# A keyed attention in a two-part network: an opening with fewer fill products and the longest tile, and token shifts moved from GpSimd into the gaps of a search on VectorE

## The chip, the cores and the metric

The kernel is one launch on one core of a Trainium2 chip. Five engines run side by side, each with its own instruction order, and meet through semaphores: TensorE (PE, matrix products into PSUM), VectorE (DVE), ScalarE (ACT), GpSimd (POOL) and SyncE (SP, which only issues transfers here). The metric is the device time of the launch in microseconds. The time before is 4012.95 us, the median of three runs (4010.0 to 4013.63).

## The reference

All arrays are float32, 1024 tokens by 1024 features. A first block (a gated mixer and an MLP) is followed by two layers of a second block, each of which runs three branches from one input product. The change touches the branch that attends to chosen keys, and the token shift of the recurrent branch, in both layers:

```python
def token_shift_mix(z, mu):
    prev = jnp.pad(z, ((0, 0), (1, 0), (0, 0)))[:, :-1]
    return z + (prev - z) * mu

# recurrent branch: r, k, v, g and two low-rank inputs are columns of z after the shift
kk = k * k_k
kk = kk / max(norm(kk, per head of 64), 1e-12)

# chosen keys, for each block of 128 queries
sc = einsum(relu(iq . ik * 32 ** -0.5), iw)         # 8 index heads of 32
sc = where(key <= query, sc, -inf)
_, idx = top_k(sc, 256)                             # the first of equal scores win
att = q . k[idx] * 64 ** -0.5                       # 4 heads of 64, one k and v for all
out = softmax(where(idx <= query, att, -inf)) . v[idx] * silu(g)
```

The kernel gathers nothing. It finds, for each query, the 256th largest score by halving an interval 32 times, makes from it a mask over all keys (0 for chosen, a huge negative number for the rest), and attends densely under the mask.

## The kernel before

Rows (tokens) lie on the 128 partitions, so there are NT = 8 tiles of 128 tokens. The phases follow each other with a barrier of all engines between them. For each of the two layers: `win2`, `dsa_attend`, `rwkv`, `dilated`, `tail`.

**`win2`, the input stage.** TensorE multiplies the normed input by twelve chunks of weight columns in the order of `WIN_CHUNKS` (L3298), 8 tiles a chunk, 8 products a tile. Most chunks are 384 columns wide, `low` is 128. Chunks 0 to 3 also feed the index scores `sc`. ScalarE evicts each tile from PSUM into one of two slots of `ot` (`evict`, L3458); a chunk may be evicted into a slot only when the chunk two before it is stored. SyncE loads the weights two chunks ahead, and for each finished chunk from 4 on stores it to DRAM (L3391). The chunks v, g, low, r and k (4, 6, 8, 9, 10) are first shifted: SyncE copies the chunk one token down into `zp` by four transfers (L3384 to L3387), and `shift` (L3340) computes z + (zp - z) * mu in three passes over the whole chunk. The first four of these run on GpSimd (L3520 to L3524), the last, k, on VectorE. ScalarE then applies SiLU to g and tanh to half of low (`shape`, L3492), at fixed places of its order.

VectorE sums the index scores (`add_heads`), and from about 1720 us of the span runs the search (`dsa_search`, L2456): a loop of BISECT = 32 trips, each with six counts over the score tiles 2 to 7 (384 to 1024 wide; tiles 0 and 1 need no choice, as all their keys are taken) and six small instructions on 128x6. Behind the search come the shift of k, the product with k_k, its square and the sum per head, then (after ScalarE's square root) the normalised `kk`, whose store closes the phase.

**`dsa_attend`, the attention.** `TILE_ORDER` is 0, 1, 7, 6, 5, 4, 3, 2; each tile has four heads, 32 units `m` in all. TensorE makes the scores of unit m + 2 (L2554), then turns unit m by transposes (L2563) and multiplies by v (L2574). VectorE adds the mask and takes the row minimum (`attend`, L2657), ScalarE takes the exponential and copies the turned blocks. The mask of a tile is made in parts: `choose` on VectorE (L2632: keys above the upper limit, candidates between the limits, a running count by a scan, the first of them up to the number needed), one part behind each unit, and the last two passes on GpSimd (L2620, L2621). `keep_busy` (L2542) issues fill products whose results are never read: 16 at the start, and 2 or 8 behind the heads of the first two tiles, 34 calls. Each call is two records in the trace, as float32 products are.

Of the kernel before, what the change touches and what calls it, by code (L numbers as in the profile page):

```python
# [2455 lines left out]
def dsa_search(ph, B, sc, junk):  # L2456
# [6 lines left out]
    def search(dve):  # L2463
        s = Steps(dve, step, 0, PRE)

# [9 lines left out]
        with dve.Fori(0, BISECT) as i:  # L2475
            s = Steps(dve, step, 0, PER)
            s.base = PRE + i * PER
# [12 lines left out]
    return search  # L2490


TILE_ORDER = list(range(T0)) + list(range(NT - 1, T0 - 1, -1))


def dsa_attend(nc, A, S, l_, hT, Z, L_, B, sc):
# [3 lines left out]
    with Phase(nc, "datt") as ph:  # L2500
        room = Z["room"]
        ident, causal = L_["ident"], B["causal"]
        gt, pre, mask = (carve(room, q * 2 * SEQ, [2, SEQ]) for q in range(3))
        cand, ones = room[:, 6 * SEQ:7 * SEQ], room[:, 7 * SEQ:8 * SEQ]
# [8 lines left out]
        ones_set, step, gstep, made, masked, expd, turned, pT_ready, o_made, inv_ready, o_read, row_done, chosen, mask_ready = (  # L2513
            ph.sem(n) for n in ("ones_set step gstep made masked expd turned pT_ready o_made inv_ready o_read row_done chosen "
                                "mask_ready").split())
# [7 lines left out]
        with ph.block() as block:  # L2523
# [17 lines left out]
            def _(pe):  # L2541
# [36 lines left out]
                def busy_after(m):  # L2578
                    i, h = m // DSA_H, m % DSA_H
                    if i < 2 and h < DSA_H - 1:  # L2580
                        keep_busy(i % 2, 8 if m == 2 * DSA_H - 2 else 2)

                scores(0)
                scores(1)
                keep_busy(0, 16)
                k = 0
                for m in range(NM):
                    if m + 2 < NM:
                        scores(m + 2)
                    while k < len(groups) and groups[k][0] == m:  # L2590
                        turn(k)
                        if k >= 1:
                            values(k - 1)
                            if groups[k - 1][0] != m:
                                busy_after(m - 1)
                        k += 1
                values(k - 1)

            @block.gpsimd
            def _(gp):  # L2600
                count = [0]

                def s(ins):
                    count[0] += 1
                    ins.then_inc(gstep, 1)
                    gp.wait_ge(gstep, START + count[0])

                gp.memset(ones[:, :], 1.0).then_inc(ones_set, 1)
                for i, t in enumerate(TILE_ORDER):
                    L, j = (t + 1) * P, i % 2  # L2610
                    mk = mask[:, j, :]
                    if i >= 2:
                        gp.wait_ge(masked, START + DSA_H * (i - 1))
                    if t < T0:
                        if t > 0:
# [1085 lines left out]
```

## Time and profile before

| | us |
|---|---|
| median of three runs | 4012.95 |
| profiled execution | 4015.7 |
| its span, first to last instruction | 4014.4 |
| TensorE busy | 3644.9 (91%) |
| VectorE busy | 2205.6 (55%) |
| ScalarE busy | 1133.7 (28%) |
| GpSimd busy | 506.2 (13%) |
| mean granted TensorE clock | 0.953 of full |

The two input stages and the two attentions take about 1565 to 2043 and 2045 to 2155 us in the first layer, 2793 to 3277 and 3279 to 3388 us in the second. In a timeline a line is the start in us, the duration in us, the engine and the line of the code, the operation, the tiles written and read, their shapes and the number of instructions merged, and in brackets the idle time of the engine before it with what ended it.

### The profile page before, as it was taken

Reading aid. Unit: us, or ns where it says so; the run is one execution under the profiler, and the core shown is the slowest. Engines: PE = TensorE matmul, PEld = TensorE weight load, DVE = VectorE, ACT = ScalarE, POOL = GpSimd, SP = SyncE. Lnnn points to the kernel's source line nnn. Section 1 sums busy time; section 2 is a strip of 40 time slices with the busy share of each in tenths; the row PEclk is TensorE's granted clock in tenths of the full one; section 3 lists DMA queues with packets and bytes.
Section 4 is the critical chain, followed back from the end, with each engine's and each line's share of the span. In section 5 each row is a group of like instructions: output and inputs, shape, how many; then the busy total and the mean of one; then the engine's idle time right before and its main releaser. Section 6 shows DMA issues by size and latency. Waiting matters only on the chain. (4 is left out here: it accounts for less than half of the span.)

```text
span 4014.4 us, 58104 instructions
## 1 busy us (share of the span) xinstructions
PE 3644.9 (91%) x22944; PEld 2327.5 (58%) x22944; DVE 2205.6 (55%) x4609; ACT 1133.7 (28%) x2429; POOL 506.2 (13%) x314
## 2 busy tenths in 40 slices
PE   5999848799999997999997997998999988898898
PEld 4555424685478544656665885444655655787444
DVE  3143476446764573589865553342389875653343
ACT  2121135221122011411134555222320114555222
POOL 0010033000110010012211111110002211121110
PEclk7999969899999998999998998999999999998899
DMA  6332322323433452123331204111013341202220
GB/s 216 137 115 88 109 101 79 116 95 147 177 117 105 147 185 86 32 63 93 111 108 50 72 20 164 49 65 57 27 56 92 105 137 52 59 30 102 94 77 23
DMA packets 234283, 377.16 MB, mean 94 GB/s; under 512 B 30742, under 2 KB 163870, under 8 KB 233014
## 3 DMA queue, kind: packets, MB, share of 16 engines
q1 hardware_dynamic: 234030, 373.58, 28.2%
q8 instruction: 184, 3.01, 0.3%
q14 instruction: 69, 0.57, 0.0%
HBM read 290.84 MB, written 69.08 MB: 90 GB/s over the span
## 5 line engine op out<-in xcount | busy, mean ns | idle before, releaser
L3413 PE MATMUL win_acc<-across_room,across_hT 128*128 128x384 f32 (+3 forms) x3072 | 907.8, 456 | 3.7 <-PEq L83 3.7
L3413 PEld LDWEIGHTS win_acc<-across_room,across_hT 128*128 128x128 f32 x3072 | 561.0, 191 | 345.1 <-issue 15.0
L2480 DVE TENSOR_SCALAR_CACHE_REDUCE win_rl<-d_sc,win_mid 128x384 f32<-128x384 f32 (+5 forms) x384 | 363.2, 946 | 35.9 <-DVE win_mid L2488 24.0
L3252 PE MATMUL tail_wo<-tail_w_out,across_room 128*128 128x512 f32 x512 | 230.1, 604 | 9.3 <-issue 9.3
L453 PE MATMUL zin_acc<-zin_wt,across_hT 128*128 128x512 f32 (+2 forms) x640 | 229.2, 513 | 0.0
L3263 PE MATMUL tail_wg<-tail_w_gate,across_room 128*128 128x512 f32 x512 | 225.3, 594 | 1.0 <-DVE across_room L3093 1.0
L3474 ACT ACTIVATE d_ot<-win_acc 128x384 f32<-128x384 f32 (+1 forms) x144 | 66.9, 466 | 562.8 <-PE win_acc L3413 562.7
L453 PEld LDWEIGHTS zin_acc<-zin_wt,across_hT 128*128 128x128 f32 x640 | 119.9, 190 | 98.3 <-issue 88.6
L3252 PEld LDWEIGHTS tail_wo<-tail_w_out,across_room 128*128 128x128 f32 x512 | 98.0, 194 | 129.0 <-issue 129.0
L1700 PE MATMUL mlp_bk<-across_hT,across_room 128*128 128x256 f32 x768 | 171.0, 379 | 0.0
L3263 PEld LDWEIGHTS tail_wg<-tail_w_gate,across_room 128*128 128x128 f32 x512 | 96.5, 191 | 116.5 <-issue 116.5
L1700 PEld LDWEIGHTS mlp_bk<-across_hT,across_room 128*128 128x128 f32 x768 | 145.9, 190 | 19.8
L3345 POOL TENSOR_TENSOR win_zp<-win_zp,d_ot 128x3072 f32<-128x3072 f32 (+1 forms) x8 | 44.8, 5605 | 824.0 <-DMA win_zp<-s_z 824.0
L2318 PE MATMUL rwkv_bk<-rwkv_Tb,rwkv_PS 64*64 64x64 f32 x1920 | 128.0, 220 | 7.6 <-DVE rwkv_PS L2075 7.6
L2316 PE MATMUL rwkv_bk<-rwkv_PS,rwkv_Tb 64*64 64x64 f32 x1536 | 113.4, 224 | 17.2 <-DVE rwkv_PS L2075 17.2
L1700 PE MATMUL mlp_bk<-mlp_tsums,mlp_sums 128*128 128x256 f32 x512 | 117.6, 383 | 10.8 <-DVE across_room L1428 9.3
L2075 DVE TENSOR_TENSOR rwkv_PS<-rwkv_bk,layer_early 128x128 f32<-128x128 f32 x240 | 67.9, 288 | 104.5 <-PE rwkv_bk L2305 103.2
L1387 POOL TENSOR_TENSOR mlp_t<-mlp_t,mlp_rows 128x1024 f32<-128x1024 f32 x8 | 20.2, 2526 | 791.8 <-ACT mlp_t L1634 791.8
L1249 PE MATMUL mid_wo<-across_room,mid_yT 128*128 128x512 f32 x256 | 113.9, 599 | 3.5 <-ACT mid_yT L1188 3.5
L2198 ACT ACTIVATE rwkv_Tb<-rwkv_bk 128x256 f32<-128x256 f32 x192 | 73.5, 383 | 150.8 <-PE rwkv_bk L2318 150.3
L3557 DVE SCALAR_TENSOR_TENSOR d_sc<-win_rl,d_iw,d_sc 128x512 f32<-128x512 f32 (+3 forms) x140 | 92.1, 658 | 41.9 <-ACT win_rl L3490 28.7
L1700 PEld LDWEIGHTS mlp_bk<-mlp_tsums,mlp_sums 128*128 128x128 f32 x512 | 98.0, 192 | 25.3 <-issue 12.0
(492 smaller groups left out, 6869.3 us busy)
## 6 DMA issues: line engine op xcount, KB each, us to landing
across_room<-in_w SPq DMA_DIRECT2D x96, 1024.0 KB, 6.9
across_room<-in_w_in SPq DMA_DIRECT2D x18, 1536.0 KB, 8.3
s_z<-d_ot SPq DMA_DIRECT2D x14, 1536.0 KB, 6.5
across_room<-in_w_ada SPq DMA_DIRECT2D x8, 2048.0 KB
across_hT<-s_z SPq DMA_DIRECT2D x16, 832.0 KB, 5.7
win_zp<-d_ot SPq DMA_DIRECT2D x8, 1344.0 KB
front_w<-in_w_ada SPq DMA_DIRECT2D x4, 2048.0 KB, 15.7
zin_wt<-in_w_in SPq DMA_DIRECT2D x4, 2048.0 KB, 9.2
```

Source lines behind the costliest of these rows:

```text
L453: mm = pe.matmul(z, w, x, start=k == 0, stop=k == KC - 1)
L1249: mm = pe.matmul(wo[:, n % 2, c, :], yT[:, n % 2, q, :], w_out[:, q, c * COL:(c + 1) * COL], start=q == 0, stop=q == KC - 1)
L1700: mm = pe.matmul(out, a[:, k, :], b[:, k, :], start=k == 0, stop=k == KC // 2 - 1)
L2075: dve.tensor_tensor(PS[:, 2 * g:2 * g + 2, :], blocks(bk[:, k % 2, 0:2 * HD]), bc_mid(levels[:, q, :], 2), ALU.mult).then_inc(p_out, 1)
L2198: act.activation(Tb[:, n % 2, g, :, :, :].rearrange("p a h t -> p (a h t)"), bk[:, 2 + k % 2, 0:4 * HD], ACT.Copy).then_inc(t_out, 1)
L2316: pe.matmul(bk[pr, 2 + k % 2, col(h)], TT_of(n, 2 * g + h, pr), PS[pr, 2 * g + h, :], start=True, stop=True)
L2318: mm = pe.matmul(bk[pr, 2 + k % 2, col(2 + h)], PS[pr, 2 * g + h, :], TT_of(n, 2 * g + h, pr), start=True, stop=True)
L2480: s(dve.tensor_scalar(junk[:, q % 2, 0:L], sc[q][:, :], mid[:, q:q + 1], 0.0, ALU.is_gt, ALU.add, accum_out=cnt[:, q:q + 1]))
L3252: mm = pe.matmul(wo[:, c, :], yT[:, n % 2, q, :], W["out"][:, q, c * COL:(c + 1) * COL], start=q == 0, stop=q == KC - 1)
L3263: mm = pe.matmul(wg[:, c, :], xT[:, n % 2, q, :], W["gate"][:, q, c * COL:(c + 1) * COL], start=q == 0, stop=q == KC - 1)
L3413: mm = pe.matmul(acc[:, u % RING, 0:w], hT[:, k, t * P:(t + 1) * P], wt[:, i % 2, k, 0:w], start=k == 0, stop=k == KC - 1)
L3557: dve.scalar_tensor_tensor(x, y, iw, x, ALU.mult, ALU.add).then_inc(summed, 1)
```

## The change

Five parts, in both layers:

1. The chunks keep their widths and places, but what they hold moves: k becomes chunk 4, v chunk 9, r chunk 10 (g stays 6, low 8).
2. GpSimd does nothing in `win2`. The search is cut at 9, 17, 21 and 25 trips, and the shifts of k, g, low and v stand in these cuts on VectorE, the shift of r behind the last trip. The product with k_k follows the shift of k.
3. Square and sum per head move to ScalarE (`norms`, six activations with an accumulator for each tile, in chunk 6). SyncE waits for them before it reuses `zp` for g.
4. VectorE makes the mask of tile 7 at the end of `win2`.
5. The attention takes the tiles as 7, 6, 5, 1, 4, 0, 3, 2. It opens with 10 fill products and has none later. While tile i is attended, VectorE makes the whole mask of tile i + 1, with the two passes that GpSimd had.

```diff
-TILE_ORDER = list(range(T0)) + list(range(NT - 1, T0 - 1, -1))
+TILE_ORDER = [7, 6, 5, 1, 4, 0, 3, 2]
...
+def choose_keys(s, dve, x, lo, hi, g, p_, cand, ones, need, mask):
+    w = x.shape[-1]
+    s(dve.tensor_scalar(g, x[:, :], hi, 0.0, ALU.is_gt, ALU.add, accum_out=need))
+    s(dve.tensor_scalar(need, need, -1.0, float(TOPK), ALU.mult, ALU.add))
+    yield
+    s(dve.scalar_tensor_tensor(cand[:, 0:w], x[:, :], lo, g, ALU.is_gt, ALU.subtract))
+    yield
+    s(dve.tensor_tensor_scan(p_, ones[:, 0:w], cand[:, 0:w], 0.0, ALU.mult, ALU.add))
+    yield
+    s(dve.scalar_tensor_tensor(p_, p_, need, cand[:, 0:w], ALU.is_le, ALU.mult))
+    yield
+    s(dve.tensor_tensor(p_, p_, g, ALU.add))
+    yield
+    s(dve.tensor_scalar(mask[:, 0:w], p_, -1.0, BIG, ALU.add, ALU.mult))
+    yield
...
-                keep_busy(0, 16)
+                keep_busy(0, 10)
...
-            @block.gpsimd
-            def _(gp):
...
-                steps = chain.from_iterable(choose(i) for i in range(T0, NT))
+                steps = iter(())
                 for m in range(NM):
                     i, h = m // DSA_H, m % DSA_H
+                    if h == 0:
+                        for _ in steps:
+                            pass
+                        steps = choose(i + 1) if i + 1 < NT else iter(())
                     attend(m)
-                    if not (i == 1 and h < 2):
+                    next(steps, None)
+                    if h < 2:
                         next(steps, None)
...
-WIN_CHUNKS = [("idx", DSA0 + 384, 296), ("qkv", DSA0, 384), ("dg", DSA0 + 680, 256), ("", DIL0, 384), ("v", 2 * RW, RW), ("", DIL0 + 384, 384),
-              ("g", 3 * RW, RW), ("", DIL0 + 768, 384), ("low", 4 * RW, P), ("r", 0, RW), ("k", RW, RW), ("gate", DIL0 + 1152, 384)]
+WIN_CHUNKS = [("idx", DSA0 + 384, 296), ("qkv", DSA0, 384), ("dg", DSA0 + 680, 256), ("", DIL0, 384), ("k", RW, RW), ("", DIL0 + 384, 384),
+              ("g", 3 * RW, RW), ("", DIL0 + 768, 384), ("low", 4 * RW, P), ("v", 2 * RW, RW), ("r", 0, RW), ("gate", DIL0 + 1152, 384)]
...
+                        if q == 1:
+                            sp.wait_ge(n6_ready, START + 1)
                         sp.dma_start(zp[1:113, :, 0:w], ot[0:112, j, :, 0:w]).then_inc(zp_in, DMA)
...
+                        if i == K:
+                            sp.wait_ge(kk_raw, START + 1)
...
+                def norms(t):
+                    for h in range(RWH):
+                        c = slice(h * HD, (h + 1) * HD)
+                        ins = act.activation(zp[:, t, c], kk[:, t, c], ACT.Square, accum_out=n6[:, t, h:h + 1])
+                    if t == NT - 1:
+                        ins.then_inc(n6_ready, 1)
...
-                gp.wait_ge(mu_in, START + (len(order) + 1) * DMA)
-                for i in order[:ON_POOL]:
-                    shift(gp, i, gstep, 0, g_shifted)
...
+                def shift(i):
+                    w = CHUNKS[i][2]
+                    q = order.index(i)
+                    z, v = ot[:, slot(i), :, 0:w], zp[:, :, 0:w]
+                    dve.wait_ge(zp_in, START + (q + 1) * 4 * DMA)
+                    d(dve.tensor_tensor(v, v, z, ALU.subtract))
+                    d(dve.tensor_tensor(v, v, bc_mid(mu[:, q, 0:w], NT), ALU.mult))
+                    dve.tensor_tensor(z, z, v, ALU.add).then_inc(mixed, 1)
+
+                prepare(dve)
+                halve(dve, 0, 9)
                 dve.wait_ge(mu_in, START + (len(order) + 1) * DMA)
...
+                shift(K)
+                dve.wait_ge(mixed, START + 1)
+                dve.tensor_tensor(kk[:, :, :], ot[:, slot(K), :, 0:RW], bc_mid(k_k, NT), ALU.mult).then_inc(kk_raw, 1)
+                halve(dve, 9, 17)
+                shift(G)
+                halve(dve, 17, 21)
+                shift(LOW)
+                halve(dve, 21, 25)
+                shift(V)
+                halve(dve, 25, BISECT)
+                shift(R)
+                d(dve.memset(ones, 1.0))
+                for _ in choose_keys(d, dve, sc[NT - 1 - T0], B["lo"][:, NS - 1:NS], B["hi"][:, NS - 1:NS], gt0, pre0, cand, ones, need, mask0):
+                    pass
```

## Rows read from the trace of the kernel before

**Rows 1.** The page, part 1: busy us (share of the span) xinstructions, TensorE

```profile
PE 3644.9 (91%) x22944; PEld 2327.5 (58%) x22944; DVE 2205.6 (55%) x4609; ACT 1133.7 (28%) x2429; POOL 506.2 (13%) x314
```

**Rows 2.** Timeline (start us, us, ...) of TensorE, joint between the stages, first layer

```profile
2044.88 0.80 PE L2554 MATMUL datt_acc<-d_kT,d_qT 64*128 64x128 f32 x4 [5.08 <-PEq L83]
```

**Rows 3.** Timeline of VectorE at the same joint

```profile
2039.61 3.36 DVE L3593 TENSOR_TENSOR d_kk<-d_kk,across_room 128x3072 f32<-128x3072 f32 x1
```

**Rows 4.** Timelines of TensorE and VectorE, the same joint in the second layer

```profile
3278.59 0.80 PE L2554 MATMUL datt_acc<-d_kT,d_qT 64*128 64x128 f32 x4 [10.32 <-PEq L83]
...
3273.15 3.36 DVE L3593 TENSOR_TENSOR d_kk<-d_kk,across_room 128x3072 f32<-128x3072 f32 x1
```

**Rows 5.** Groups by line, VectorE, 1720:2018: group | busy us, mean ns | idle

```profile
L2484 DVE COPY_PREDICATED d_lo<-win_ge,win_mid 128x6 f32<-128x6 uint8 x32 | 26.2, 818 | 4.7 <-DVE win_lt L2482 0.2
...
L2486 DVE COPY_PREDICATED d_hi<-win_lt,win_mid 128x6 f32<-128x6 uint8 x32 | 24.8, 774 | 4.7
...
L2481 DVE TENSOR_SCALAR win_ge<-win_cnt 128x6 uint8<-128x6 f32 x32 | 15.7, 491 | 1.1
...
L2482 DVE TENSOR_SCALAR win_lt<-win_cnt 128x6 uint8<-128x6 f32 x32 | 5.6, 174 | 1.1
```

**Rows 6.** Timeline of VectorE, first counts: trips 1, 10; second layer's trip 1

```profile
1720.41 0.61 DVE L2480 TENSOR_SCALAR_CACHE_REDUCE win_rl<-d_sc,win_mid 128x384 f32<-128x384 f32 x1 [0.24 <-DVE win_cnt L2473]
...
1790.06 0.61 DVE L2480 TENSOR_SCALAR_CACHE_REDUCE win_rl<-d_sc,win_mid 128x384 f32<-128x384 f32 x1 [0.37 <-DVE win_mid L2488]
...
2948.87 0.61 DVE L2480 TENSOR_SCALAR_CACHE_REDUCE win_rl<-d_sc,win_mid 128x384 f32<-128x384 f32 x1 [0.23 <-DVE win_cnt L2473]
```

**Rows 7.** Timeline of GpSimd, first pass of shifts, chunks 4 and 9, two layers

```profile
1793.96 6.67 POOL L3345 TENSOR_TENSOR win_zp<-win_zp,d_ot 128x3072 f32<-128x3072 f32 x1 [236.47 <-DMA win_zp<-s_z]
...
1973.75 6.70 POOL L3345 TENSOR_TENSOR win_zp<-win_zp,d_ot 128x3072 f32<-128x3072 f32 x1 [40.40 <-DMA win_zp<-s_z]
...
3199.84 6.68 POOL L3345 TENSOR_TENSOR win_zp<-win_zp,d_ot 128x3072 f32<-128x3072 f32 x1 [36.17 <-DMA win_zp<-s_z]
```

**Rows 8.** Timeline of SyncE's queue around the copy of chunk 9

```profile
1957.27 0.38 SPq L3305 DMA_DIRECT2D across_room<-in_w_in  x1
...
1960.35 0.43 SPq L3387 DMA_DIRECT2D win_zp<-s_z  x1
```

**Rows 9.** Timeline of ScalarE: last eviction of chunk 6; an activation with accumulator

```profile
1860.42 0.49 ACT L3474 ACTIVATE d_ot<-win_acc 128x384 f32<-128x384 f32 x1 [4.67 <-PE win_acc L3413]
...
2046.51 0.40 ACT L2690 ACTIVATE datt_att<-datt_att,datt_nm 128x128 f32<-128x128 f32 x1 [0.38 <-DVE datt_nm L2657]
...
2046.82 0.19 ACT L2690 ACTIVATION_READ_ACCUMULATOR datt_att<-datt_att,datt_nm 128x1 f32 x1
```

**Rows 10.** Groups by shape, VectorE, 2044:2160; last line: instructions of one line

```profile
L2642 DVE SCALAR_TENSOR_TENSOR across_room<-d_sc,d_lo,across_room 128x1024 f32<-128x1024 f32 x1 | 1.3, 1282 | 0.0
...
L2644 DVE TENSOR_TENSOR_SCAN across_room<-across_room 128x1024 f32<-128x1024 f32 x1 | 2.3, 2289 | 0.0
...
L3122 DVE TENSOR_TENSOR across_room<-across_room x16: 1224/1224/1226, 2575.9 to 4005.2; 128x1024 f32<-128x1024 f32 x16
```

**Rows 11.** Timeline of TensorE: first 16 and last 8 fill products, first layer

```profile
2045.61 9.03 PE L2544 MATMUL datt_po<-d_g,d_v 128*128 128x256 f32 x32
...
2070.59 3.67 PE L2544 MATMUL datt_po<-d_g,d_v 128*128 128x256 f32 x16
```

**Rows 12.** Stretch 2074.20:2153.80, all engines: PE PEld DVE ACT POOL, PEclk, DMA, GB/s

```profile
2074.20:2153.80 79.60, 77.47 (x473) 56.49 (x472) 39.05 (x86) 39.33 (x84) 9.79 (x10) 1.00 0.03 11
```

**Rows 13.** Stretches of 1 us, the same columns

```profile
2042.00:2043.00 1.00, 0.00 (x0) 0.00 (x0) 0.96 (x1) 0.00 (x0) 0.00 (x0) 0.79 0.00 0
...
2049.00:2050.00 1.00, 1.00 (x5) 0.83 (x5) 0.40 (x1) 0.00 (x0) 0.00 (x0) 0.80 0.97 273
```

**Rows 14.** Timeline of TensorE, scores of two heads one behind the other

```profile
2083.11 1.77 PE L2554 MATMUL datt_acc<-d_kT,d_qT 64*128 64x512 f32 x4
...
2087.51 1.77 PE L2554 MATMUL datt_acc<-d_kT,d_qT 64*128 64x512 f32 x4
```

More of the change, by code:

```diff
@@ L2502, in dsa_attend @@
         ident, causal = L_["ident"], B["causal"]
-        gt, pre, mask = (carve(room, q * 2 * SEQ, [2, SEQ]) for q in range(3))
-        cand, ones = room[:, 6 * SEQ:7 * SEQ], room[:, 7 * SEQ:8 * SEQ]
+        gt0, pre0, cand, ones, mask0 = choosing_buffers(room)
+        mask = [mask0, room[:, 3 * SEQ:4 * SEQ]]
         need = ph.sb("need", [P, 1])
@@ L2512, in dsa_attend @@
         po = ph.ps("po", [P, 2, 512])
-        ones_set, step, gstep, made, masked, expd, turned, pT_ready, o_made, inv_ready, o_read, row_done, chosen, mask_ready = (
-            ph.sem(n) for n in ("ones_set step gstep made masked expd turned pT_ready o_made inv_ready o_read row_done chosen "
-                                "mask_ready").split())
+        step, made, masked, expd, turned, pT_ready, o_made, inv_ready, o_read, row_done = (
+            ph.sem(n) for n in "step made masked expd turned pT_ready o_made inv_ready o_read row_done".split())
         stored = [ph.sem("stored0"), ph.sem("stored1")]
@@ L2593, in _ @@
                             values(k - 1)
-                            if groups[k - 1][0] != m:
-                                busy_after(m - 1)
                         k += 1
                 values(k - 1)
-            @block.gpsimd
-            def _(gp):
[L2601 to L2615, printed above, removed]
-                            s(gp.memset(mk[:, 0:t * P], 0.0))
-                        gp.tensor_copy(mk[:, t * P:L], causal[:, :]).then_inc(mask_ready, 1)
-                        continue
-                    gp.wait_ge(chosen, START + i - T0 + 1)
-                    s(gp.tensor_tensor(mk[:, 0:L], pre[:, j, 0:L], gt[:, j, 0:L], ALU.add))
-                    gp.tensor_scalar(mk[:, 0:L], mk[:, 0:L], -1.0, BIG, ALU.add, ALU.mult).then_inc(mask_ready, 1)
             @block.vector
@@ L3311, in win2 @@
     NCH, LOCAL, RING = len(CHUNKS), 3, 3
-    SHIFTED = ("v", "g", "low", "r", "k")
-    ON_POOL = 4
-    order = [i for i, c in enumerate(CHUNKS) if c[0] in SHIFTED]
+    order = [i for i, c in enumerate(CHUNKS) if c[0] in ("v", "g", "low", "r", "k")]
     shapes = [i for i in order if CHUNKS[i][0] in ("g", "low")]
-    G, LOW, R, K = (next(i for i, c in enumerate(CHUNKS) if c[0] == n) for n in ("g", "low", "r", "k"))
+    G, LOW, R, K, V = (next(i for i, c in enumerate(CHUNKS) if c[0] == n) for n in ("g", "low", "r", "k", "v"))
     slot = lambda i: i if i < 2 else (i - LOCAL) % 2
@@ L3513, in _ @@
                             shape(G)
-                        if i == R and t == 3:
+                        if i == LOW + 1 and t == 3:
                             shape(LOW)
+                        if i == K + 2 and t >= 1:
+                            act.wait_ge(kk_raw, START + 1)
+                            norms(t - 1)
+                            if t == NT - 1:
+                                norms(t)
                         if i == NCH - 1 and t == NT - 3:
```

97 lines of the change are left out of this document (35 added, 62 removed).

## The prediction

> **What bounds the kernel now.** I read the page first: TensorE is busy 91% of the span, so a change on other engines pays only where TensorE waits [rows 1]. Then I took the two stages that the change touches, in both layers: `win2` (the input products, with the search for the 256 chosen keys beside them) and `dsa_attend`. The timeline of TensorE shows one unbroken run of products to 2039.80 us and then 5.08 us of nothing before the attention [rows 2]. In the second layer the gap is 10.32 us [rows 4]. The timeline of VectorE says what ends it: the last instruction of the input stage is the product on `kk` (L3593), over at 2042.97 and, in the second layer, at 3276.51 [rows 3, 4]. TensorE starts about 2 us behind it each time [rows 2, 4]. So the input stage is bound by TensorE for 99% of its length, and VectorE sticks out by 3.2 us in the first layer and 8.3 us in the second. Inside the attention TensorE is the bound again: 77.47 us busy of 79.60 once the long tiles run [rows 12].
>
> **What the shifts on GpSimd cost now.** One trip of the search takes (1790.06 - 1720.41) / 9 = 7.74 us [rows 6]. 32 such trips are 247.6 us. The search takes longer, since it stalls while GpSimd shifts: three small instructions on six columns average 0.82, 0.77 and 0.49 us over the 32 trips where a fourth of the same size takes 0.17, which is 20.7 + 19.2 + 10.1 = 50 us above it [rows 5]. The counts over up to 1024 columns aren't slowed. All this goes.
>
> **What comes back on VectorE.** A pass over 128x3072 takes 3.36 us there, 3.4 with the step to the next [rows 3], against about 6.7 on GpSimd [rows 7]. A shift is three passes, 10.2 us. VectorE gets v, g and r (30.6) and `low`, a third as wide (some 3.7): 34.3 us for the 50 that it loses. The squares and the sum of `kk` leave it for ScalarE (-6.8). So by busy time alone VectorE gains 22 us a layer, and spends 9.7 of it on choosing the keys of tile 7 (below). Busy time isn't what decides, though.
>
> **The wait that the change adds.** Each shift now stands in VectorE's own order and waits for the shifted copy of a chunk, which is read back only once TensorE has finished that chunk. GpSimd's starts show when these copies land [rows 7]; the widths of the chunks stay in the same order, so TensorE's clock of chunks and the copies stay where they are. Queued behind each such wait is the whole rest of the search, and behind that the start of attention. In order, first layer: nine trips end at 1790.1, the first copy is there at 1793.96 (3.9 lost). Its shift and `kk` take 13.6, eight trips 61.9, giving 1869.9 with the loop's entry. For the next copy, that of `g`, SyncE must now also wait for the norms on ScalarE before it may overwrite `zp`. The chunk's last tile is evicted near 1860.9 [rows 9], and 12 norms follow. A 128x128 activation with its accumulator read takes 0.50 us [rows 9]; 64 columns a little less, so 12 cost 5 to 6 us. With 12 to 16 us from issue to landing (`v`'s took 16) the copy is there between 1878 and 1883. That loses 8 to 13, but nobody pays, because the later waits absorb it: VectorE would reach the shift of `v` (25 trips done) at about 1961, while the copy of that chunk, issued right behind a weight load of 1957.3 and complete at SyncE by 1960.8 [rows 8], lands at 1973.75 [rows 7]. The end therefore hangs on this one landing, whatever came before. In the second layer VectorE is there at about 3192, and the copy lands at 3199.84.
>
> From the landing on, everything is VectorE's own work:
> shift v 10.2; seven trips 7 x 7.74 = 54.2 and about 1.0 for entering and leaving the loop; shift r 10.2 (its copy is there long before); then tile 7's choice. Three passes over 1024 columns at 1.28 with their steps are 4.0, the scan 2.3, the add 1.25 [rows 10], the small one 0.2. The memset and the last scaling have no row on VectorE at this size; nothing and two passes of 1.28 bound them, and I put 1.9 for both, near the upper end, as they go over the same columns: 9.6 in all. The norm's maximum and reciprocal take 0.7, the last product 3.4. The sum is 89.3 us.
> First layer: 1973.8 + 89.3 = 2063.1, against 2042.97, so +20.1. Second: 3199.8 + 89.3 = 3289.1, against 3276.5, so +12.6. Together 32.7 us later. TensorE ends where it did (2039.8 and 3268.3) and then idles some 25 us. Bounds: if copies land 2 us earlier or the loop's joints are free, 27; if each of the joints costs 1 us more, 37. SyncE's other stores keep their room: `k` is stored earlier than `v` was, the store of g still hangs on the SiLU in ScalarE's order behind tile 5 of the next chunk. The norms, 6 x 0.5 = 3 us a tile, fit into the 4.7 us that ScalarE idles between two evictions, so TensorE isn't held up.
>
> **The attention.** Of 34 fill products a layer 10 stay. In records, 68 become 20. The first 32 took 9.03 us, 16 at full clock 3.67, that is 0.23 each [rows 11]; the five fours between come to 4.6. Out go 9.03 + 4.6 + 3.67 = 17.3, in come 20 x 0.23 = 4.6: a gain of 12.7. Nothing hid behind them that is still needed: tiles 0 and 1 were filled out while the masks of tile 7 were made. Against it stands the clock. It falls to 1.2 GHz near 2042.8, three us into the gap, and is back at 2.4 GHz near 2049.2, 4.3 us after TensorE starts [rows 13]. Today these 4.3 us fall on fill products; then they fall on the scores of the long tile, and half of them, 2.2 us, is lost. Last, VectorE takes over GpSimd's two mask passes: some 2.1 us for 1024 columns, less for others. Over a long tile it has, with a masked reduction priced like a pass and 1.1 for the output rows, 4 x 1.3 + 9.7 + 1.1 = 16 us of work against TensorE's 4 x 4.4 = 17.6 [rows 14], which fits. Beside tiles 1 and 0 it doesn't: scaled by the widths, an estimate, 8.4 and 7.2 us against TensorE's 4.7 and 3.4, 7.5 us too much. But VectorE runs up to two heads ahead, so I put 1.2 there, with 0 and 7.5 as the ends. Gain a layer: 12.7 - 2.2 - 1.2 = 9.3 (3 to 10.5, or 12.7 if the clock costs nothing); two layers 18.6 (6 to 25).
>
> **The sum.** +32.7 - 18.6 = +14.1 us. The profiled execution took 4015.7 (span 4014.4), the median of the runs is 4012.95. On the median that is 4027.
>
> **A rule against a row.** The rows show GpSimd's passes stalling small VectorE instructions, and that the stalls outweigh what VectorE takes over by 50 - 34.3 = 16 us a layer [rows 5]; that gives rival A. The Trainium skill, "SBUF — State Buffer", part "SBUF: two separate sides", calls the port pair that the two engines share an exclusive lock held for a whole instruction. The trace agrees; by this rule alone the change should win, since GpSimd falls silent in the stage. My sum goes against it because it ends in a DMA's landing, not in busy time.
>
> **The rivals.**
> A, faster: the copies do not hold VectorE. Without any wait VectorE's work after 1720.4 is 247.6 + 13.6 + 34.3 + 9.6 + 4.1 + some 5 for joints = 314 us. It would end at 2035, before TensorE (2039.8), and at 3263, before 3268. The stage then ends with TensorE, -3 and -8, and with the attention's 18.6 the time is 4013 - 30 = 3983. For it: the stalls are real. Against: the landings in [rows 7]. It decides only if all four copies are there when VectorE comes. Chance 0.06.
> B, about the same: the mechanism holds, but the copy of `v` lands earlier than GpSimd's start says, or the attention gives back the full 12.7. A copy of `v` that VectorE never waits for leaves ends of 1961 + 89.3 = 2050 and 3281, +12 instead of +32.7, so 4007; half of that wait gone is 4017. So 4007 to 4020. Chance 0.22.
> C, much slower: with 10 fills after 25 us of idling the clock stays at 1.2 GHz through tile 7, 17.6 us a layer more: 4062. Against: today the clock is back after 4.3 us of dense work [rows 13], and what stands there after the change, scores, fills, transposes, is dense too. The Trainium skill, "TensorE: Matmul & The Clock Gate", Part 1, says the default is throttled and activity releases it, which speaks for the recovery. Chance 0.04.
> D: the forecast, 4027, own range 4014 to 4040. Chance 0.68.
>
> **How the numbers follow.** The range 4009 to 4040 takes in D and most of B; A and C stay outside, a tenth. A measurement of this kernel tells some 0.2%, 8 us, from no change. Slower by more than that (over 4021) holds nearly all of D and C: 0.70. Within: nearly all of B and D's low end, 0.23. Faster: A and a little of B, 0.07.
>
> **What would show it.** Right: in the profile after, VectorE idle before the first pass of the fourth shift on `zp` from about 1961 to 1974, released by the DMA; `kk`'s last product ending near 2063 and 3289; TensorE idle about 25 and 23 us before L2554's first product; a trip of 7.74 us throughout; the attention 9 us shorter. Wrong: a TensorE gap of 5 us or less (A), an attention stage at half clock (C), gaps of TensorE beside tiles 1 and 0 of several us (the 7.5), or a shift of g that comes so late that the evictions of chunk 8 wait.

## The result and the profile after

The changed kernel takes 4047.52 us (median of 4 runs, 4045.63 to 4050.16) against 4013.29 for the kernel before beside it: a ratio of 1.0086, 95% interval 1.0069 to 1.0104, so 34 us more. The direction was forecast, the size was not: the forecast was 4027, range 4009 to 4040.

The table is worked out from TensorE's timelines: each stage from the first product in it to the first of the next, the attention to its own last product. "Falls" is how long after the attention's start the granted clock leaves 1.00 for good in that stage; "the end" is within 3 us of its last product, or behind it.

| profiled execution | input stage 1 | attention 1 | input stage 2 | attention 2 | falls |
|---|---|---|---|---|---|
| before, span 4014.4 | 479.8 | 108.9 | 485.4 | 109.9 | at the end |
| after, span 4045.5 | 499.2 | 112.5 | 497.2 | 112.3 | 81, 80 us |

The input stages give +19.4 and +11.8 us and the attentions, with their joints to the next stage, +3.2 and +2.4. What lies ahead of the first input stage, an unchanged part, was 5.1 us shorter in this execution, and the rest of the program differs by less than 2: together the +31.1 of the two spans.

VectorE's timeline of the changed kernel: the first pass of the shift of `v` (in brackets the idle time before it and what ended it) and the last product on `kk`, in both layers. They answer [rows 3, 4]:

```profile
1968.46 3.36 DVE L3574 TENSOR_TENSOR win_zp<-win_zp,d_ot 128x3072 f32<-128x3072 f32 x1 [12.62 <-DMA win_zp<-s_z]
...
2053.92 3.36 DVE L3599 TENSOR_TENSOR d_kk<-d_kk,layer_early 128x3072 f32<-128x3072 f32 x1
```

```profile
3216.02 3.36 DVE L3574 TENSOR_TENSOR win_zp<-win_zp,d_ot 128x3072 f32<-128x3072 f32 x1 [9.92 <-DMA win_zp<-s_z]
...
3300.61 3.36 DVE L3599 TENSOR_TENSOR d_kk<-d_kk,layer_early 128x3072 f32<-128x3072 f32 x1
```

Counted from the start of its stage, `v` lands 408.5 us in, against 408.7 in [rows 7]: the landing stayed put, as the prediction said, and VectorE stood there for 12.6 us. From it to the end are 2057.28 - 1968.46 = 88.8 us (89.3 forecast). TensorE's first product of the attention in both layers answers [rows 2, 4], with the gap ahead of it:

```profile
2059.19 3.79 PE L2576 MATMUL datt_acc<-d_kT,d_qT 64*128 64x512 f32 x8 [24.46 <-PEq L83]
...
3305.99 3.79 PE L2576 MATMUL datt_acc<-d_kT,d_qT 64*128 64x512 f32 x8 [22.20 <-PEq L83]
```

The stalls of VectorE are gone: the two instructions that averaged 0.82 and 0.77 us in [rows 5] are these groups now (busy, mean ns):

```profile
L2485 DVE COPY_PREDICATED d_lo<-win_ge,win_mid 128x6 f32<-128x6 uint8 x32 | 5.5, 171 | 4.7
L2487 DVE COPY_PREDICATED d_hi<-win_lt,win_mid 128x6 f32<-128x6 uint8 x32 | 5.5, 171 | 4.7 <-DVE d_lo L2485 0.2
```

What no step of the sum foresaw lies in the attention. TensorE's timeline behind tile 0:

```profile
2138.44 1.12 PE L2576 MATMUL datt_acc<-d_kT,d_qT 64*128 64x512 f32 x2 [0.68 <-DVE datt_nm L2641]
2139.49 0.33 PE L2585 MATMUL datt_tp<-layer_ident,datt_att 128*128 128x128 f32 x1
2139.66 0.33 PE L2596 MATMUL datt_po<-d_v,datt_pT 128*128 128x64 f32 x2
2139.92 2.07 PE L2576 MATMUL datt_acc<-d_kT,d_qT 64*128 64x512 f32 x2
```

The same product, tile 3's scores of one head, takes 1.12 us, and one head later it takes 2.07. The stretches around it (us, busy PE, PEld, DVE, ACT, POOL, granted clock, DMA share, GB/s):

```profile
2134.00:2140.00 6.00, 4.92 (x30) 3.40 (x28) 4.80 (x14) 2.71 (x11) 0.00 (x0) 1.00 0.07 22
2140.00:2156.00 16.00, 16.00 (x43) 9.32 (x43) 7.54 (x21) 5.94 (x15) 0.00 (x0) 0.50 0.03 9
2156.00:2171.60 15.60, 15.60 (x61) 12.63 (x60) 2.57 (x9) 4.45 (x11) 0.00 (x0) 0.50 0.03 8
```

The attention ran at 2.4 GHz until 2140 and then at 1.2 to its end, though TensorE was busy without a break. From the slow scores product at 2139.92 to the last product the work of tiles 3 and 2 took 31.7 us. Where the clock held (e16_rows_late, below) it took 17.2 from the same product on, so 14.5 us were lost, in each layer.

### The profile page after: what moved, and what is told of

It reads as the page before. It is cut to its first block and busy times, and to the rows that moved or that the text cites. A ratio compares the mean times of both kernels' runs of the same rounds, so it can differ in the third digit from the quotient of the medians.

```text
span 4045.5 us, 58056 instructions
## 1 busy us (share of the span) xinstructions
PE 3648.1 (90%) x22848; PEld 2330.4 (58%) x22848; DVE 2172.8 (54%) x4661; ACT 1157.6 (29%) x2621; POOL 339.0 (8%) x258
## 5 line engine op out<-in xcount | busy, mean ns | idle before, releaser
L3251 PEld LDWEIGHTS tail_wg<-tail_w_gate,across_room 128*128 128x128 f32 x512 | 96.6, 191 | 116.4 <-issue 116.4
L1987 POOL TENSOR_TENSOR rwkv_be<-rwkv_b,rwkv_f 128x384 f32<-128x384 f32 x16 | 20.3, 1270 | 1686.5 <-DVE rwkv_yo L2033 1362.5
L2576 PE MATMUL datt_acc<-d_kT,d_qT 64*128 64x512 f32 (+3 forms) x192 | 90.2, 621 | 48.6 <-PEq L83 46.7
L2316 PE MATMUL rwkv_bk<-rwkv_PS,rwkv_Tb 64*64 64x64 f32 x1536 | 113.6, 225 | 17.2 <-DVE rwkv_PS L2075 17.2
L1700 PE MATMUL mlp_bk<-mlp_tsums,mlp_sums 128*128 128x256 f32 x512 | 118.6, 386 | 9.7 <-DVE across_room L1428 9.3
L1700 PEld LDWEIGHTS mlp_bk<-mlp_tsums,mlp_sums 128*128 128x128 f32 x512 | 98.8, 194 | 24.4 <-issue 10.9
```

The lines of the kernel that those rows point to most:

```text
L1700: mm = pe.matmul(out, a[:, k, :], b[:, k, :], start=k == 0, stop=k == KC // 2 - 1)
L2316: pe.matmul(bk[pr, 2 + k % 2, col(h)], TT_of(n, 2 * g + h, pr), PS[pr, 2 * g + h, :], start=True, stop=True)
L2576: mm = pe.matmul(acc[:, m % 2, c // COL, 0:w], B["qT"][pr, h // 2, t * P:(t + 1) * P], B["kT"][pr, c:c + w], start=True, stop=True)
L3251: mm = pe.matmul(wg[:, c, :], xT[:, n % 2, q, :], W["gate"][:, q, c * COL:(c + 1) * COL], start=q == 0, stop=q == KC - 1)
```

## The experiments

All start from the changed kernel. Each was timed beside the kernel before, and the ratio is to that. This is the table of stages again, with the medians:

| kernel | us (ratio, 95%) | input 1, 2 | attention 1, 2 | falls |
|---|---|---|---|---|
| e1_cuts | 4004.3 (0.9968 to 0.9987) | 476.7, 476.9 | 111.0, 111.4 | 76, 80 |
| e2_order | 4026.4 (1.0019 to 1.0047) | 499.6, 497.0 | 100.8, 100.7 | 95, 94 |
| e3_fills | 4043.5 (1.0062 to 1.0096) | 499.6, 497.1 | 107.0, 108.0 | the end |
| e6_input_only | 4028.7 (1.0020 to 1.0045) | 492.0, 489.7 | 108.5, 109.5 | the end |
| e5_cuts_order | 3976.2 (0.9890 to 0.9923) | 476.6, 477.5 | 96.7, 96.6 | the end |
| e7_cuts_order_nofill | 4107.6 | 477.2, 476.9 | 162.7, 163.4 | 5, 1 |
| e8_tile1_mid | 4024.2 (1.0017 to 1.0038) | 500.1, 497.5 | 99.6, 99.2 | the end |
| e9_fills1 | 4052.7 (1.0067 to 1.0118) | 498.9, 497.0 | 120.9, 118.6 | 74, 77 |
| e10_cuts_tile0_last | 3978.1 (0.9896 to 0.9929) | 476.4, 476.9 | 96.6, 98.7 | the end |
| e11_cuts_order_5fills | 3974.4 (0.9888 to 0.9921) | 477.1, 476.9 | 97.4, 96.4 | 90, the end |
| e12_tile0_mid | 4079.6 (1.0147 to 1.0180) | 498.4, 497.4 | 127.1, 126.8 | 58, 59 |
| e13_0fills | 4152.6 (1.0242 to 1.0369) | 499.0, 497.9 | 163.2, 163.5 | 7, 7 |
| e14_no_choice_4_3 | 4048.0 (1.0068 to 1.0102) | 499.3, 497.4 | 112.3, 112.1 | 81, 80 |
| e15_fills_tile0 | 4039.2 (1.0050 to 1.0084) | 499.8, 497.5 | 103.6, 103.4 | the end |
| e16_rows_late | 4018.3 (1.0004 to 1.0023) | 499.1, 497.6 | 96.9, 96.3 | the end |
| e17_best_rows_late | 3972 to 4037 | 476.5, 476.9 | 159.8, 94.8 | 11, the end |
| e18_cuts_rows | 3992.2 (0.9933 to 0.9966) | 476.7, 476.9 | 111.9, 95.8 | 73, the end |
| e19_all_three | 3968.2 (0.9874 to 0.9907) | 476.7, 476.9 | 94.9, 96.5 | the end |

**The landings.** If VectorE's end hangs on the wait for `v`, trips of the search put ahead of the waits remove the gap. This run also asks whether the half clock is an after-effect of that gap.

```diff
-                halve(dve, 17, 21)
+                halve(dve, 17, 23)
                 shift(LOW)
-                halve(dve, 21, 25)
+                halve(dve, 23, 28)
                 shift(V)
-                halve(dve, 25, BISECT)
+                halve(dve, 28, BISECT)
```

> The changed kernel, with the search cut after trips 9, 17, 23 and 28 in place of 9, 17, 21 and 25. In the changed kernel VectorE idles 13.5 us before the shift of low and 12.6 us before that of v (14.1 and 9.9 us in the second layer); now trips of 7.74 us stand there. Landing theory: VectorE's end falls to 1968.5 + 10.2 + 4 x 7.74 + 1 + 10.2 + 9.4 + 4.0 = 2034 us in the first layer (2057.3 now) and 3282 in the second (3304), TensorE's gap ahead of the attention shrinks from 24.5 and 22.2 us to 2 to 6, so some 37 us less than the changed kernel: 4011. Two theories of the half clock late in the attention part here. Thin tiles: it falls because of the short tiles 1 and 0 in the middle, so it falls in this kernel too, some 80 us after the attention's start, and the time is 4011. Long gap: it is an after-effect of TensorE's 25 us of idling, so it stays at full speed here, 12 to 14 us a layer less on top: 3985.

The input stages shrink by 22.6 and 20.3 us and the median by 43.2. VectorE's timeline shows the shifts of `low` and `v`, then the last product, and TensorE's the fall:

```profile
1925.32 1.23 DVE L3574 TENSOR_TENSOR win_zp<-win_zp,d_ot 128x1024 f32<-128x1024 f32 x1 [0.21 <-DVE win_mid L2489]
1970.44 3.36 DVE L3574 TENSOR_TENSOR win_zp<-win_zp,d_ot 128x3072 f32<-128x3072 f32 x1 [3.07 <-DMA win_zp<-s_z]
...
2032.24 3.36 DVE L3599 TENSOR_TENSOR d_kk<-d_kk,layer_early 128x3072 f32<-128x3072 f32 x1
```

```profile
2114.52 2.07 PE L2576 MATMUL datt_acc<-d_kT,d_qT 64*128 64x512 f32 x2 [0.68 <-DVE datt_nm L2641]
```

The landing theory holds, and VectorE's work now ends before TensorE's, as rival A had it; only the places of the cuts stood between the change and that gain. The long gap is gone as well (1.8 us), and yet the clock falls behind tile 0. So the fall is no after-effect of the gap.

**The input stage alone**, with the attention stage of the kernel before (old tile order, fills, masks on GpSimd) and without the choice at the end:

```diff
-TILE_ORDER = [7, 6, 5, 1, 4, 0, 3, 2]
+TILE_ORDER = list(range(T0)) + list(range(NT - 1, T0 - 1, -1))
...
-                d(dve.memset(ones, 1.0))
-                for _ in choose_keys(...):
-                    pass
```

> The changed kernel's input stage (shifts on VectorE, its order of chunks, its cuts) without the choice of tile 7's keys at its end, followed by the attention stage of the kernel before, with its tile order, its fills and its masks on GpSimd. It prices the input stage alone. Landing theory: VectorE ends 9.4 us earlier than in the changed kernel, at 2047.9 - so +10.0 and +2.4 us against before, the attention takes what it took before (113.6 and 114.6 us with its joint to the next stage), so 4013 + 12 = 4025, and the rest of the changed kernel's loss is the attention's. Thin tiles: the clock is full through the attention, as in before. Long gap: after 15 us of idling in place of 5 the clock falls late in the attention here too, 10 us a layer or more: 4045.

It takes 4028.7: 12.2 and 4.3 us more in the input stages than before, attentions of 108.5 and 109.5 at full clock. The landing theory had 4025. Of the changed kernel's +31.2 us in the input stages, 16.5 are the shifts' and their waits', and 14.7 the choice's on VectorE (499.2 - 492.0 and 497.2 - 489.7).

**Where the short tiles stand.** Three other tile orders, each with one more wait of VectorE, for its own last masked reduction, ahead of the masks of tiles 1 and 0. Every later run that moves tiles or output rows has this wait too, and so has e14_no_choice_4_3:

```diff
-TILE_ORDER = [7, 6, 5, 1, 4, 0, 3, 2]
+TILE_ORDER = [7, 6, 5, 4, 3, 2, 1, 0]
...
+                    dve.wait_ge(masked, START + DSA_H * (i - 1))
```

> The changed kernel with the tiles of the attention in the order 7, 6, 5, 4, 3, 2, 1, 0, so that the two short tiles stand last, with no other change of the work (one wait of VectorE for its own last masked reduction ahead of the masks of tiles 1 and 0). Thin tiles: tiles 4, 3 and 2 run at full clock, and whatever falls, falls in the last 6 to 8 us; the attention takes 99 to 102 us in place of 112.5, so 4024 in place of 4047.5. Long gap: the clock falls some 80 us after the start as in the changed kernel, with tile 3 or 2, and the attention takes 107 or more: 4037 to 4048.

The same line with `[7, 6, 5, 1, 4, 3, 2, 0]`:

> The changed kernel with the tile order 7, 6, 5, 1, 4, 3, 2, 0: tile 1 stays in the middle, tile 0 goes to the end. In the changed kernel the clock holds at 2.4 GHz through tile 1 and falls 1 to 2 us behind tile 0. If it takes both short tiles, the clock stays up until the last few us here: attention 101 to 103 us, 4025 to 4030. If tile 1 alone is enough and only its effect is late, the clock falls some 80 us after the start also here: attention 110 to 112, 4042 to 4048. (With both short tiles last the measured attention was 100.8 us and the time 4026.4.)

And with `[7, 6, 5, 0, 4, 3, 2, 1]`:

> The changed kernel with the tile order 7, 6, 5, 0, 4, 3, 2, 1: now tile 0 alone stands in the middle. With tile 1 alone there the clock held, attention 99.4 us, time 4024.2; with both it fell at 78 to 81 us, 112.4 us, 4047.5. If it takes both, the clock holds here too: attention 99 to 102, 4023 to 4029. If tile 0 is the one that does it, the clock falls with tile 4 or just behind it, at some 60 to 70 us, and more work runs at half speed than in the changed kernel: attention 118 to 130, 4060 to 4080.

It is tile 0's place that decides here. With it at the end the clock lasts through all long tiles, tile 1 in the middle or not (100.8 and 99.6 us). With it alone in the middle the clock falls 58 and 59 us in, and 68 to 69 us run at half speed. These are stretches of the last two kernels:

```profile
2128.00:2159.00 31.00, 29.50 (x180) 21.35 (x179) 16.53 (x48) 15.84 (x43) 0.00 (x0) 1.00 0.04 13
```

```profile
2112.00:2118.00 6.00, 5.07 (x36) 4.13 (x35) 4.28 (x11) 1.76 (x6) 0.00 (x0) 0.99 0.01 3
2118.00:2187.00 69.00, 68.31 (x216) 47.21 (x216) 23.35 (x67) 21.65 (x59) 0.00 (x0) 0.50 0.03 10
```

**Fill products beside the short tiles.** Behind the first three heads of a tile, in three doses:

```diff
+                def busy_after(m):
+                    i, h = m // DSA_H, m % DSA_H
+                    if TILE_ORDER[i] < T0 and h < DSA_H - 1:
+                        keep_busy(i % 2, 4)
...
                             values(k - 1)
+                            if groups[k - 1][0] != m:
+                                busy_after(m - 1)
```

> The changed kernel with four fill products behind each of the first three heads of tiles 1 and 0, 24 a layer, 0.23 us each at full clock, 5.5 us of TensorE's time, part of it in its waits there. Thin tiles: the density beside the short tiles is restored, the clock stays at 2.4 GHz through tiles 3 and 2, 14 us a layer are back for 4 to 5.5 spent: attention 102 to 104 us, 4029. Long gap: the clock falls all the same, and the fills are added on top: 4055 to 4059.

One in place of four:

> The changed kernel with one fill product, in place of four in the run before, behind each of the first three heads of tiles 1 and 0: 6 a layer, 12 records of 0.23 us, 2.8 us at most. With four the clock stayed at 2.4 GHz to the end of the attention, but the attention took 107.0 us (112.5 with none). If one is enough: 99 to 102 us, 4023 to 4029. If it isn't: the clock falls at 80 us as without, attention 112 to 115, 4047 to 4053.

Four, beside tile 0 only:

> The changed kernel with four fill products behind each of the first three heads of tile 0 only: 12 a layer, 24 records of 0.23 us, 5.5 us. Filled beside both short tiles (11 us of fills) the profiled attention took 107 to 108 us at full clock. If tile 0 alone needs it: 112.5 - 14.5 + 5.5 less 1 us of waits covered, 102 to 104 us, 4026 to 4031. If the clock falls all the same: 115 to 120 us, 4053 to 4065.

Four hold the clock to the end in the profiled execution, beside tile 0 alone too. The first expectation has an error of mine: a fill is two records, so 24 fills are 48 records and 11 us, not 5.5, and 112.5 - 15 + 11 less 1 to 2 of covered waits is the 107 measured. The median of that run, 4043.5, is 10 us above its profiled execution (4033.4), so in other executions some clock was lost again; where, no trace shows. One fill doesn't help: in the profiled execution the fall comes 6 and 3 us earlier than without and the fills run at half speed too, but over four executions (4042 to 4063 us) the time can't be told from the 4047.5 without. Bought in this way the clock costs most of what it gives (4039.2 at best).

**What in tile 0's stretch does it.** Two candidates on VectorE: the choice of keys beside it, and the output rows, behind which the masked scores wait that TensorE waits 0.68 us for.

```diff
+                    if t in (3, 4):
+                        return
                     if t >= T0:
```

> The changed kernel with VectorE's choice of the keys of tiles 4 and 3 left out (their masks hold what stood there before, so part of the computation is missing): 6 us less of VectorE's work beside tile 1, 4.9 beside tile 0. The prediction feared VectorE's lateness there, 0 to 7.5 us. If that lateness is what makes TensorE thin and lowers the clock, the clock holds and the time is 4018 to 4024. If not, 4044 to 4049, and the choice costs nothing on the path.

```diff
-                    if h == 1 and i >= 1:
+                    if h == 3 and i >= 1:
                         rows_out(i - 1)
```

> The changed kernel with the output rows of a tile written by VectorE behind the fourth head of the next tile, not behind the second. In the changed kernel VectorE waits 0.96 us beside tile 0 for the products of tile 4 and passes over its output rows, then makes the masked scores of tile 0's third head, and TensorE waits 0.68 us for these, just ahead of the fall of the clock. If that wait brings on the fall, the clock holds at 2.4 GHz to the end here, attention 97 to 99 us, 4018 to 4023. If the short products of tile 0 do it by themselves, the clock falls at 78 to 81 us all the same: attention 111 to 113, 4044 to 4049.

Leaving out some 11 us of VectorE's work a layer changes nothing, so the choice beside the short tiles costs nothing on the path either (4048.0; falls at 81 and 80). TensorE's wait ahead of the fall is still there, 0.62 us. Moving the output rows two heads later gives 29 us: 4018.3, within 0.2% of the kernel before. The added wait of VectorE isn't what does it, since the clock falls with it in e14_no_choice_4_3 and in e12_tile0_mid. TensorE's timeline at the same place, and the stretches around it:

```profile
2138.55 0.33 PE L2585 MATMUL datt_tp<-layer_ident,datt_att 128*128 128x128 f32 x1
2138.72 0.33 PE L2596 MATMUL datt_po<-d_v,datt_pT 128*128 128x64 f32 x2
2138.98 1.12 PE L2576 MATMUL datt_acc<-d_kT,d_qT 64*128 64x512 f32 x2
```

```profile
2135.60:2141.60 6.00, 5.60 (x29) 3.38 (x29) 5.19 (x14) 3.12 (x12) 0.00 (x0) 1.00 0.01 3
2141.60:2157.60 16.00, 16.00 (x101) 11.74 (x101) 9.47 (x28) 9.56 (x25) 0.00 (x0) 1.00 0.08 25
```

The wait is gone, and 16 us hold 101 records of products, nearly as many as the 31.6 us behind tile 0 in the changed kernel (43 and 61).

**Do the causes add, and does the wait explain all?** First the cuts with the order 7 to 0:

> The changed kernel with both edits, the search cut after trips 9, 17, 23 and 28, and the tiles in the order 7 to 0. If the two losses are independent (the landings of the copies, and the half clock caused by the short tiles in the middle), their gains add: 4047.5 - 43.2 (the cuts alone) - 21.2 (the order alone) = 3983, by stages 476.7 and 476.9 us to the attention's start, and attentions of 99 to 101 us. If one loss covered the other (an attention that starts warm has less to gain), 3990 to 4004.

The cuts with tile 0 alone last:

> The changed kernel with the search cut after trips 9, 17, 23 and 28, and the tiles in the order 7, 6, 5, 1, 4, 3, 2, 0: tile 1 in the middle, where alone it did not lower the clock, tile 0 last. With the order 7 to 0 and these cuts the time was 3976.2 us, and without the cuts tile 0 alone at the end gave an attention 1.2 to 1.5 us shorter than both short tiles at the end. If these add: 3973 to 3974. If tile 1 in the middle is on the edge and the clock falls here: some 12 us a layer more, 3990 to 4000.

The cuts with the late rows, in the change's own tile order:

> The changed kernel with the cuts after trips 9, 17, 23, 28 and the output rows behind the fourth head; its tile order and its ten fills are kept. If the landings and the wait behind the output rows are the two causes and independent: 4047.5 - 43.2 - 29.2 = 3975. If an attention that starts warm gains less, as with the order 7 to 0, 3976 to 3982. If the clock is lost beside tile 0 after all, 3990 to 4004.

All three edits:

> The same with the tiles in the order 7 to 0 on top. With cuts and this order alone the time was 3976.2, and with late rows and six fills the second layer's attention took 94.8 us (96.6 without late rows) in a profile whose first layer had lost the clock at the opening. If ten fills hold it: attentions of 95 to 97 us, 3973 to 3976, with no execution above 3985. If late rows themselves endanger the opening, some executions at 4030 or more.

The landings and the tile order add, and a little more: 3976.2 where the sum was 3983. The traces show where from: the attention now starts at full clock and takes 96.6 us, against 100.8 in e2_order, where it started at half. Moving tile 1 as well or not makes no difference (3978.1). The late rows don't add as cleanly: 3992.2 in place of 3975. In the first layer of that profile the clock falls inside tile 4's last products beside tile 0, with no wait for VectorE near it:

```profile
2103.39 1.10 PE L2596 MATMUL datt_po<-d_v,datt_pT 128*128 128x64 f32 x8 [0.40 <-ACT datt_pT L2684]
...
2106.18 1.90 PE L2596 MATMUL datt_po<-d_v,datt_pT 128*128 128x64 f32 x8 [0.40 <-ACT datt_pT L2684]
```

In its second layer, the same instructions, it holds. The profiled execution (3981.4) is the fastest of four, and the others (3992 to 3994) are longer by about what one more layer would lose; no trace shows them. So without VectorE's wait the clock held in one setting and not in the other: the wait isn't the whole condition. With tile 0 last as well, nothing is at stake, and the kernel takes 3968.2 us, 1.1% less than the kernel before (ratio 0.9890).

**The opening.** The prediction counted every fill taken out as time won. The kernel with cuts and order 7 to 0, with no fill, and with five:

```diff
-                keep_busy(0, 10)
```

> The same with no fill product at the attention's opening (the changed kernel has 10, 20 records of 0.23 us). The prediction counted each fill product taken out as time won. If that holds to the last one, the attention loses another 4 to 4.6 us a layer against the kernel with both edits: some 8 us less in all. If TensorE would only idle in their place, waiting for the first masked scores and their exponentials, the time is the same within 2 us; and if the thin opening lets the clock fall or stay low, it is 5 to 20 us longer.

> The kernel with both edits (cuts 9, 17, 23, 28; tiles 7 to 0; 3976.2 us) with 5 fill products at the attention's opening in place of 10. With none the clock fell 4 us after the attention's start and stayed at 1.2 GHz to its end, 66 us a layer. If only the bridging of TensorE's waits for the first masked scores counts, 5 products (10 records of 0.23, 2.3 us) close the first wait of 1.3 us and nearly the second, and the time is 2 to 4 us less: 3972 to 3974. If the opening needs all ten, the clock falls: 4040 to 4110.

The changed kernel itself with none:

> The changed kernel with no fill product at the opening, the tile order and the cuts as they are in it. Here the attention starts at 1.2 GHz after TensorE's gap of 24.5 us, and with ten fills the clock is back after 5 us. This is the prediction's rival C in a sharper form. If the scores and transposes of tile 7 are dense enough at half clock to bring it back, the time is 4040 to 4048. If the fills are what brings it back, the whole attention runs at half clock, 163 to 168 us in place of 112.5: 4140 to 4160.

And all three edits with six:

> The changed kernel with the cuts after trips 9, 17, 23, 28, the tiles in the order 7 to 0, 6 fill products at the opening and the output rows behind the fourth head. The same with 5 fills and the rows behind the second head took 3974.4 us, attentions 96.4 and 97.4. If the late rows take the small waits away (0.3 to 0.9 us a tile, some 3 us a layer at most) 3968 to 3973. If TensorE then waits elsewhere, for the output rows ahead of the next tile's products, the same within 2 us: 3973 to 3977.

Without fills the attention runs at half clock from 1 to 7.5 us behind its start to its end, in both settings: 163 us. This is TensorE's timeline of the first of them, with waits of 1.8, 1.3 and 1.5 us; the clock falls at 2044.4, so behind the second wait and ahead of the third:

```profile
2039.34 1.99 PE L2576 MATMUL datt_acc<-d_kT,d_qT 64*128 64x512 f32 x8 [1.81 <-PEq L83]
2042.62 2.07 PE L2576 MATMUL datt_acc<-d_kT,d_qT 64*128 64x512 f32 x4 [1.28 <-DVE datt_nm L2641]
2044.62 1.97 PE L2585 MATMUL datt_tp<-layer_ident,datt_att 128*128 128x128 f32 x8
2048.08 1.97 PE L2596 MATMUL datt_po<-d_v,datt_pT 128*128 128x64 f32 x8 [1.49 <-ACT datt_pT L2683]
2049.98 3.78 PE L2576 MATMUL datt_acc<-d_kT,d_qT 64*128 64x512 f32 x4
```

With ten (e5_cuts_order) it starts so, and the clock stays:

```profile
2038.25 1.99 PE L2576 MATMUL datt_acc<-d_kT,d_qT 64*128 64x512 f32 x8 [1.81 <-PEq L83]
2040.18 4.58 PE L2566 MATMUL datt_po<-d_g,d_v 128*128 128x256 f32 x20
2044.69 1.98 PE L2576 MATMUL datt_acc<-d_kT,d_qT 64*128 64x512 f32 x4
2046.60 1.09 PE L2585 MATMUL datt_tp<-layer_ident,datt_att 128*128 128x128 f32 x8
2047.95 1.10 PE L2596 MATMUL datt_po<-d_v,datt_pT 128*128 128x64 f32 x8 [0.25 <-ACT datt_pT L2684]
```

Five held in four executions (3973.3 to 3978.3). Six, with the late rows, held in six of twelve (3972 to 3981) and failed in the other six (4031 to 4037), so no median stands for that kernel. The late rows have no part in this: the first rows that they move are written 27 us into the attention in the kernel with five, and the clock falls 11 us in. Up to there the two kernels differ in one fill. This is TensorE behind the opening with five, and then with six, in the profiled execution that lost the clock:

```profile
2048.31 1.10 PE L2596 MATMUL datt_po<-d_v,datt_pT 128*128 128x64 f32 x8 [1.46 <-ACT datt_pT L2684]
2049.34 1.98 PE L2576 MATMUL datt_acc<-d_kT,d_qT 64*128 64x512 f32 x4
```

```profile
2045.51 1.10 PE L2596 MATMUL datt_po<-d_v,datt_pT 128*128 128x64 f32 x8 [1.02 <-ACT datt_pT L2684]
2046.54 2.41 PE L2576 MATMUL datt_acc<-d_kT,d_qT 64*128 64x512 f32 x4
```

The longer wait kept the clock and the shorter one lost it, so with five the four good executions may be luck. The 2 us that fewer fills save aren't worth it. One execution without fills took 4045 and one 4103 where their fellows took 4108 and 4153, 63 and 49 us less, about what one layer's attention at full clock saves.

## Why the prediction was right and wrong

- **The stalls go.** Right: both groups are at 0.17 us, and GpSimd's busy time fell from 506 to 339 us.
- **The wait for `v` sets the end of the stage.** Right in place and size: landings as in [rows 7], 88.8 us behind them for 89.3, TensorE's gaps 24.5 and 22.2 for "some 25 and 23", stages +19.4 and +11.8 for +20.1 and +12.6. The memset and the scaling took 0.91 and 0.69 us, 1.6 for the 1.9 put down. The copy of `g` came 5 to 10 us sooner than forecast: the norms held SyncE back by some 3 us only, and the copy took 8.6 us from its first issue (1858.79) to VectorE's start (1867.36) where 12 to 16 were put down. As said, nobody pays or gains.
- **Rival B, a copy of `v` that nobody waits for.** It wasn't so. With other cuts VectorE still waits 3.1 us for the copy, but TensorE doesn't, and that pays more than B had it (e1_cuts).
- **The attention gives back 9.3 us a layer.** This is the step that failed. It lost 3.6 and 2.4 instead, a miss of 12 to 13 us a layer and 25 in all; with it in the sum the forecast would have been 4052, and 4047.5 was measured. The cold start was priced about right: 2.2 us (2.3, if [rows 13] are read exactly: the clock is back at 2049.4) for the 2.8 and 2.4 that half of the first 5.7 and 4.7 us come to. The other terms were fair too: with tile 0 last the attention is 8.1 and 9.2 us shorter than before (e2_order), with the late rows 12.0 and 13.6 (e16_rows_late). What failed is "against it stands the clock": I charged 2.2 us for a cold start at the opening and, beside tiles 1 and 0, 1.2 us of waits by their length. The waits were of that size (0.27 and 0.68 for VectorE), but behind them the clock was lost for all the rest of the stage, which cost 14.5 us; without that loss the attention would have been 10.9 and 12.1 us shorter than before. The old order had both short tiles ahead of everything with fills between their heads; I read these fills as padding for the masks of tile 7. Going by e15_fills_tile0, where fills beside tile 0 keep the clock, they may have kept it too; no run takes them out of the old order.
- **Rival C, half clock.** It had the right kind of loss, at another place of the stage, and 0.04. I asked whether the clock comes back at the opening, found the answer in [rows 13], and didn't ask where else in the stage TensorE would be thin. The opening itself is nearer the edge than "dense too" said: without the fills the clock came back on the scores alone, 3 to 4 us after the start, and was lost again 7 us after it, behind one wait of 1.3 us (e13_0fills). The Trainium skill, "TensorE: Matmul & The Clock Gate", section "A second HAM failure mode: psum-queue depth-cycling", tells of a kernel whose clock was lost to short idles between groups of products. The trace agrees in part: behind the opening TensorE waited seven times before the fall, 0.18 to 0.68 us each. But here the clock fell once and stayed down, and with five of these waits (0.18 to 0.40 us, e16_rows_late) it held.

What stays open: which measure of TensorE's work in the stretch around tile 0 decides. In the changed kernel the fall comes right behind the wait of 0.68 us, and with late output rows the wait and the fall are both gone. But in e18_cuts_rows (first layer) and in e9_fills1 the clock falls 73 to 77 us in, with no wait for VectorE ahead of it that is longer than 0.15 us. That the short tiles' thin work costs the clock is shown by the orders, the fills and the late rows; that this one wait is the cause is not.

## What to carry over

Price a wait of TensorE by the work that stands behind it in the stage, not by its length: put the thinnest work last, where nothing is left to slow down, and take fill products out only with an eye on the granted clock. When one engine's work is laid between arrivals of transfers, read the arrivals from the trace, divide their distances by the length of a trip and cut there: the same instructions with other cuts were worth 43 us here. And run a kernel near such an edge many times, since it can come out in two groups.

## What the runs showed of the hardware

- TensorE's clock fell to 1.2 GHz in a stage where, once it had begun, TensorE never idled longer than 0.7 us, and then stayed there for 31.7 us (68 in e12_tile0_mid; 156 in e13_0fills, behind a wait of 1.3 us) while TensorE was busy nearly without a break. The dense scores, transposes and value products of tiles 4, 3 and 2 did not bring it back there, though at the opening it came back within 4 us on the scores of tile 7 alone (e13_0fills).
- A few fills can be of no use: with one behind each of six heads the clock fell 6 and 3 us earlier in the profiled execution than without, and the time was no better.
- The longest wait doesn't tell where the clock is lost: behind one of 1.46 us it held (e11_cuts_order_5fills), behind one of 1.02 at the same place it fell (e17_best_rows_late).
- The same instructions in the same kernel kept the clock in one layer and lost it in the other (e17_best_rows_late, e18_cuts_rows), and a kernel at the edge came out in two groups 55 us apart.
